# The mixer's indexer and recurrence, moved into the projections and the attention

## The reference, cut to what matters

```python
h = modulate(rmsnorm(x, mix_pre_g), m[3], m[4])
proj = h @ w_in
q, k, v, q_idx, k_idx, w_idx, x_lru, g_lru = split(proj)
# indexer: 8 heads of 64
score = einsum(relu(q_idx @ k_idx.T * 64 ** -0.5), w_idx * 8 ** -0.5)
score = where(admissible, score, -inf)        # causal by chunks of 64
top_idx = top_k(score, 64)                    # the keys each query may see
attn = softmax(q @ k.T / 8 + rel_bias, over the kept keys) @ v      # 8 heads of 64
# recurrence
xc = conv4(x_lru); r = sigmoid(xc @ w_a + b_a); i = sigmoid(xc @ w_i + b_i)
log_a = -8 * r * softplus(-lam); a = exp(log_a)
b = sqrt(-expm1(2 * log_a)) * i * xc
lru = scan(h = a * h + b) * gelu(g_lru)
merged = concat(rmsnorm(attn, attn_out_g), rmsnorm(lru, lru_out_g))
y = merged @ w_out
```

## Time and profile before

| what | us |
|---|---|
| median of 3 runs (3625.7 to 3627.49) | 3626.76 |
| the profiled execution's own time | 3632.07 |
| its span, first to last instruction | 3630.3 |
| projections' last product ends (start of span = 0) | 361.4 |
| attention's first product starts | 433.2 |
| output product starts | 482.5 |

### The profile page before, as it was taken

How to read it: one execution, slowest core, us unless ns; L and a number is a source line. 1 busy time by engine, 2 the same in 40 slices (tenths; PEclk the granted TensorE clock), 3 DMA queues, 4 the chain that set the end, 5 groups by cost and what they waited for, 6 DMA issues and landing times. The chain is left out here.

```text
span 3630.3 us, 55207 instructions
## 1 busy us (share of the span) xinstructions
PE 3347.6 (92%) x21195; PEld 3042.9 (84%) x21195; DVE 2466.5 (68%) x4014; ACT 1434.9 (40%) x1693; POOL 1078.2 (30%) x670
## 2 busy tenths in 40 slices
PE   6999479999798999989999999999988999999999
PEld 5989269957466899989999999997768999998887
DVE  5864737766575199998848998985663977106665
ACT  5433324312343333356633333323233457544443
POOL 0110000010000068766664334540000975660000
PEclk9999579989999999999999999998999999999999
DMA  7964026642002267789999999992103658867875
GB/s 297 337 244 180 0 93 223 241 151 103 24 1 90 73 210 265 255 271 364 362 328 402 378 378 410 409 356 82 58 24 140 213 189 254 266 224 283 304 281 210
DMA packets 305195, 814.35 MB, mean 224 GB/s; under 512 B 21760, under 2 KB 188928, under 8 KB 253696
## 3 DMA queue, kind: packets, MB, share of 16 engines
q1 hardware_dynamic: 241856, 583.07, 45.0%
q0 software_dynamic: 58752, 213.94, 15.8%
q10 hardware_dynamic: 4416, 15.05, 1.1%
HBM read 722.84 MB, written 89.13 MB: 224 GB/s over the span
## 5 line engine op out<-in xcount | busy, mean ns | idle before, releaser
L2521 POOL TENSOR_TENSOR arena_split<-ring,arena_split 128x1024 fp32r<-128x1024 f32 x256 | 643.5, 2525 | 1015.3 <-ACT arena_split L2475 1014.4
L2548 PE MATMUL ps<-xT_split,arena_split 128*128 128x384 f32 (+1 forms) x4096 | 916.6, 312 | 19.3 <-POOL arena_split L2521 11.4
L2548 PEld LDWEIGHTS ps<-xT_split,arena_split 128*128 128x128 f32 x4096 | 697.7, 191 | 20.3 <-issue 17.5
L2548 PE MATMUL ps<-hT_split,arena_split 128*128 128x384 f32 (+1 forms) x2048 | 635.1, 310 | 0.0
L2865 PE MATMUL ps<-arena_split 128*128 128x384 f32 x3072 | 535.7, 335 | 12.2 <-DVE arena_split L2817 12.1
L2865 PEld LDWEIGHTS ps<-arena_split 128*128 128x128 f32 x3072 | 534.2, 188 | 13.8 <-issue 12.0
L284 DVE TENSOR_TENSOR arena_split<-ring,arena_split 128x2048 fp32r<-128x2048 f32 x128 | 292.6, 2292 | 318.7 <-ACT arena_split L278 318.3
L2790 ACT ACTIVATE arena_split<-ring 128x2048 fp32r<-128x2048 f32 x128 | 245.5, 1918 | 477.1 <-PE ps L2865 282.7
L2548 PEld LDWEIGHTS ps<-hT_split,arena_split 128*128 128x128 f32 x2048 | 392.2, 191 | 0.0
L278 ACT ACTIVATE arena_split<-ring 128x2048 fp32r<-128x2048 f32 x128 | 244.0, 1912 | 351.0 <-PE ps L813 133.3
L2814 DVE TENSOR_TENSOR arena_split<-ring,arena_split 128x2048 fp32r<-128x2048 f32 x128 | 293.1, 2290 | 103.9 <-ACT arena_split L2790 103.7
(11 more groups left out here) (317 smaller groups left out, 5361.1 us busy)
## 6 DMA issues: line engine op xcount, KB each, us to landing
ring<-in_weights SPq DMA_DIRECT2D x396, 1024.0 KB, 5.3
arena<-in_side_weights POOLq DMA_DIRECT2D x152, 512.0 KB, 5.9
gates<-arena SPq DMA_DIRECT2D x48, 512.0 KB, 9.5
arena<-gates SPq DMA_DIRECT2D x32, 768.0 KB, 12.8
arena<-activations SPq DMA_DIRECT2D x64, 384.0 KB, 10.7
activations<-arena SPq DMA_DIRECT2D x128, 128.0 KB, 2.9
gates<-arena SPq DMA_DIRECT2D x16, 1024.0 KB, 6.9
arena<-gates SPq DMA_DIRECT2D x64, 256.0 KB, 5.0
```

The lines of the kernel that those rows point to most:

```text
L2521: pool.tensor_tensor(low, self.raw(f)[:, j, :], high.bitcast(F32), ALU.subtract)\
L2548: mm = pe.matmul(k.ps[:, j, 0:self.T], self.u[:, 2 * (f % 2) + j, a, t * P:(t + 1) * P], self.h[b][:, t, :], start=n == 0, stop=n == 3 * D ...
```

## The change

**The projections** take the chunks in the order 7, 8, 6, 4, 5, 9, 10, 0, 1, 2, 3: the recurrence's input, the indexer's keys, weights and queries, the gelu's input, and last q and k. SyncE loads them in that order, and the tiles of `proj` are renumbered. The loops over chunks are written out. On ScalarE `high(c + 2)` now stands ahead of the copy of chunk c. Behind chosen chunks each engine gets a slot of other work (c counts positions in the new order):

- TensorE: after c = 4 to 7 four indexer products each (after 4 also the small transposes), after c = 8 the eight gate products, into PSUM banks 4 to 7, which the projections do not use.
- ScalarE: the small exponential after c = 2, four relus each after 4 to 7, sigmoids after 8 and 9, the gelu after 10. It also copies v out, and then does tanh and exponential (`decays`).
- VectorE: half of the convolution behind `low(3)` and `low(4)`, softplus behind `low(5)`, four multiply-adds behind `low(6)` to `low(9)`, the rounds of largest values spread from `low(9)` on, and after `low(12)` the gates' scaling. Its last work in the stage is 3 rounds and the mask.

The relus have four buffers where they had two. The recurrence's tiles move to arena column 23040, the indexer's to 6656.

**The attention** takes the rest of the recurrence: VectorE does one piece at the end of steps 0, 1, 6, 7 to 10 (one scan of 256 columns each) and 11; ScalarE the square root after unit 6 and the squares after unit 14; TensorE the products with ones after the last unit. **TurnNormed** has the root, the reciprocal and the last four multiplications, and its end is signalled by VectorE after ScalarE's copies. The two stages Recurrence and Indexer are gone from the list.

```diff
 class Projections(Stage):
...
+    ORDER = (7, 8, 6, 4, 5, 9, 10, 0, 1, 2, 3)
...
+        for c in range(EARLY, self.CHUNKS):
             w.wait(pe, c)
-            pe.wait_ge(self.copied.sem, c + self.copied.at(-1))
+            pe.wait_ge(self.copied.sem, self.copied.at(c - 1))
...
+            if 4 <= c < 8:
+                pe.wait_ge(self.copied.sem, self.copied.at(c))
+                if c == 4:
+                    self.index.turn(pe)
+                self.index.products(pe, c - 4)
+            elif c == 8:
+                self.lru.gate_products(pe, self.index)
...
+        for c in range(self.CHUNKS):
+            w.wait_used(act, c)
+            w.high(act, c + 2, c + 2)
+            act.activation(self.proj[:, 2 * c:2 * c + 2, :].rearrange("p a t -> p (a t)"), k.ps[:, c % 2, :],
+                           ACT.Copy).then_inc(self.copied.sem, 1)
...
+        for c in range(EARLY, self.CHUNKS + 2):
+            w.low(dve, c, c)
+            if c in (3, 4):
+                dve.wait_ge(self.copied.sem, self.copied.at(c - 2))
+                lru.convolve(dve, c - 3)
+            elif c == 5:
+                lru.softplus(dve)
+            elif 6 <= c < 10:
+                index.add(dve, c - 6)
+                if c == 9:
+                    index.best_of(dve, 0, 0, 2)
+            elif c == 10:
+                index.best_of(dve, 0, 2, 6)
+            elif c == 11:
+                index.best_of(dve, 0, 6, 8)
+                index.best_of(dve, 1, 0, 2)
+            elif c == 12:
+                index.best_of(dve, 1, 2, 5)
+                lru.scale_gates(dve)
+        index.best_of(dve, 1, 5, 8)
+        index.mask(dve)
...
 class Recurrence:
...
+    def vector(self, dve, step):
+
+        t, chain = self.t, self.chain
+        if step == 0:
+            dve.wait_ge(self.acts.sem, self.acts.at(4))
+            chain(dve.tensor_tensor(t["sq"], t["a"], t["a"], ALU.mult))
+        elif step == 1:
+            dve.scalar_tensor_tensor(t["b"], t["sq"], 1.0, t["b"], ALU.add, ALU.mult).then_inc(self.steps.sem, 1)
+        elif step == 6:
+            dve.wait_ge(self.acts.sem, self.acts.at(5))
+            chain(dve.tensor_tensor(t["b"], t["b"], t["i"], ALU.mult))
...
+    def scalar(self, act, u):
+
+        t = self.t
+        if u == 6:
+            act.wait_ge(self.steps.sem, self.steps.at(3))
+            act.activation(t["b"], t["b"], ACT.Sqrt).then_inc(self.acts.sem, 1)
...
 class TurnNormed(Stage):
...
+        self.lru.out(dve)
+        self.finish(dve, (self.moved, 1))
```

More of the change, by code:

```diff
@@ L1001, in __init__, with begin @@
         self.sp = k.small[:, 16:64].rearrange("p (a b) -> p a b", b=4)
[L1003 to L1020, removed]
+    def begin(self, dve):
+        sp, lam = self.sp, self.k.col("lam")
+        chain = self.chain = Chain(dve, self.dve_chain)
         chain(dve.tensor_scalar(sp[:, 0, :], lam, -1.0, None, ALU.mult))
@@ L1036, in vector, with gate_products, sigmoids, gelu @@
         chain(dve.tensor_scalar(sp[:, 9, :], sp[:, 9, :], -8.0, None, ALU.mult))
+    def gate_products(self, pe, index):
+        k, t = self.k, self.t
+        pe.wait_ge(self.conv.sem, self.conv.at(1))
+        pe.wait_ge(k.late_load.sem, k.late_load.at(48))
+        pe.wait_ge(index.relus.sem, index.relus.at(16))
+        for g in range(2):
+            for c in range(4):
+                mm = pe.matmul(k.ps[:, 4 + 2 * g + c // 2, (c % 2) * SEQ:(c % 2 + 1) * SEQ], k.lru_w[:, g, c, :],
+                               t["xc"][:, c, :], start=True, stop=True)
+        mm.then_inc(self.gates.sem, 1)
+    def sigmoids(self, act, g):
+        k = self.k
+        if g == 0:
+            act.wait_ge(self.gates.sem, self.gates.at(1))
+        out, bias = self.t["ri"[g]], ("b_a", "b_i")[g]
+        for c in range(4):
+            last = act.activation(out[:, c, :], k.ps[:, 4 + 2 * g + c // 2, (c % 2) * SEQ:(c % 2 + 1) * SEQ], ACT.Sigmoid,
+                                  bias=k.col(bias, c, 1))
+        if g:
+            last.then_inc(self.acts.sem, 1)
+    def gelu(self, act):
+        act.activation(self.t["gelu"], self.gl, ACT.Gelu_apprx_tanh).then_inc(self.acts.sem, 1)
+    def scale_gates(self, dve):
+        t, sp = self.t, self.sp
         dve.wait_ge(self.acts.sem, self.acts.at(2))
@@ L1052, in vector @@
                 chain(ins)
[L1053 to L1059, removed]
@@ L1192, with __init__ @@
 class Attention(Stage):
-    def __init__(self, k, units, at, scale=None, turn=None, turned=None):
+    def __init__(self, k, units, at, scale=None, turn=None, turned=None, beside=None):
+        self.beside = beside
         self.k, self.s, self.units, self.scale, self.turn, self.buf = k, k.stage(), units, scale, turn, turned
@@ L1297, in tensor @@
                 value(step)
+        if self.beside:
+            self.beside.tensor(pe)
     def scalar(self, act):
@@ L3016, in program @@
         second_rest = turn(3, (2, 3, 4, 5), 7, layer=(1, 1))
+        lru = Recurrence(k)
         stages = [
@@ L3054, in _ @@
             def _(sp):
+                mixer = FIRST["w_in"]
                 def load(c, slot):
```

258 lines of the change are left out of this document (140 added, 118 removed).

## The result

The changed kernel takes 3572.84 us (median of 4 runs, 3569.48 to 3577.87) where the kernel before takes 3627.12 (4 runs): ratio 0.985 with a 95% interval of 0.983 to 0.986. Timed again in five rounds it took 3569.15, ratio 0.984 (0.982 to 0.985). Forecast were 3573.7 us, in a range of 3567.5 to 3582.5.

A forecast was written before the change was run, and what follows sets the result against it. TensorE sets the projections' pace, VectorE the serial recurrence and indexer. Attention starts 53.3 us earlier, the end loses 0.15: -53.1 takes the profiled 3632.07 to 3579.0, or 3573.7 after the 5.3 us median difference; range 3567.5 to 3582.5.

The forecast's parts named there:

- Index products: TensorE's 32 indexer passes, moved into the projections, add 7.2 us there, and the two small transposes 0.4.
- lower bound of 6.4: Least time for the index products in the projections: 32 passes at 0.20 us each, at 2.4 GHz.
- Gate products: TensorE's gate products, moved into the projections, take 3.4 us there, against 6.42 at the low clock; upper bound 6.4.
- Start: Chunk 2's first product comes at 296.4 instead of 296.90, gaining 0.5 us; the half clock up to 300 stays.
- Slots: Work behind each chunk fits the engines' free time, stalls zero; tightest `low(6)` and `low(12)`, about half a us to spare.
- the rival of the leaking slots: Projections: late `low` stalls TensorE 1 to 2 us, half clock adds 2.9; three slots cost 13, 3587; chance 0.1.
- Tail: VectorE's last run, from `low(11)` to the mask, takes 22.7 us; attention starts at 379.9 instead of 433.2, gaining 53.3.
- Attention: The recurrence's pieces beside the attention cost 0, bounds 0 and 12.1 us; it starts at 1.2 GHz as before.
- The rival's upper bound: Attention takes the pieces one behind the other: up to 8.5 + 3.6 = 12.1 us return, 3585.8; chance 0.08.
- End: After the attention, VectorE's last multiplications run beside transposes and ScalarE's moves; signalling through VectorE loses 0.15 us.
- The rival, given 0.2: Output product starts at full clock, raised by the products with ones: 2.5 us returns, 3571.2; chance 0.2.
- Sum: Whole program: -53.3 + 0.15 = -53.1 us, so the profiled 3632.07 us becomes 3579.0 and the median 3573.7.

The follow-up runs named there:

- The second profile of before: The kernel before, unchanged, once more under the profiler: 3620.86 us in its one run, 239.93 us from the early products' end to the feed-forward.

## Why the prediction was right

**What bounds.** TensorE's pace in the projections and VectorE's last run behind them, as forecast: with softplus doubled TensorE's wait passed on in full, and with the rounds placed earlier the attention came 6.4 us sooner.

**Index products.** Forecast 7.2 + 0.4 with the transposes, measured 1.47 + 3 x 1.25 = 5.2, 2.4 less. This is the term that was mis-sized, and it lies under the lower bound of 6.4. The bound took the time of a full-height pass for each; alternating heads lie on different halves of the partitions, and their passes overlap.

**Gate products.** Forecast 3.4, measured 3.44.

**Start.** Forecast 0.5 us earlier and the half clock kept as a cost; the gap was 1.54 us (c = 2 at 296.53) and the clock stayed at 1.00, which the profile of before had lost by chance. That is 1.5 us too little in the forecast against that profile, and none against an ordinary execution of before.

**Slots.** Forecast at no cost, and measured so. `low(6)` ended 2.3 us ahead of chunk 6's first product (317.72 + 2.29 against 322.29) and not half a us: I had counted VectorE's lateness, but not all of the time that the index products and transposes give. In the rival of the leaking slots, the price of a half clock was read wrong: chunk 2 ran at 0.50 for 3.1 us and lost 1.5, not 2.9. The real price of one late `low` is in the run with softplus twice, a stall of 2.85 and 1.6 of clock.

**Tail.** VectorE's last run was forecast at 22.7 us from `low(11)`; it took 22.2 (353.67 to 375.9). The terms named for it add up to 22.5.

**Attention.** Pieces at no cost: measured 0.14. The page on table loads of the Trainium skill (ScalarE: Activation LUTs, What ACT_TABLE_LOAD costs) would have added a drain of 1380 ns to each switch; the trace disagrees, with 1.31 us from the end of one function to the start of the next (389.80 to 391.11 and 392.17 to 393.48), of which the load is 1.28. The rival's upper bound was added too high: the pieces on VectorE are 4 x 1.22 + 2.44 = 7.3 us and not 8.5, so 10.9 in place of 12.1. What I missed is that the table which `decays` loads stays for the attention, 1.15 us.

**End.** Forecast 0.15 lost, measured 0.30 gained. The transposes at full clock gave 0.87, but the output product starts 2.23 us behind them where it started 1.66 behind them before: 0.57 lost. The forecast had VectorE's last multiplications run beside ScalarE's copies, and they end 0.5 us after them. Where the transposes were slow, with softplus twice, the copies ended last again and the signal cost 0.13, as forecast.

**The output product's clock.** The rival, given 0.2, came half true: the product began at 1.00 and fell to 0.50 after about 1.2 us. But 29.58 can't be called a gain of the change: with the products with ones it took 29.45 to 30.53 in seven profiles, without them 29.86 and 29.87, and in three profiles of the old order 29.53, 30.01 and 30.59.

**Sum.** Forecast 53.1. Against the first profile of before, the differences are 2.4 of index products, 0.4 of the tail, 1.5 of chunk 2's clock, 1.15 of the table, 0.45 at the end and 1.0 of the output product: 60.0, and the mixer measures 59.9. The second profile of before had kept chunk 2's clock, made the gate products in 1.0 less and the output product in 0.6 less: that takes 3.1 off, and 56.9 is what it measures. So the path and the overlaps were right, and the gain was put 3.8 us too low. That the time was forecast within 1 us of the first median is luck: 3626.76 less 56.9 would be 3569.9, near the second median, and the first lay 3.7 us above the second by the spread of stages that the change doesn't touch.

## What to carry to other kernels

When a serial stretch is moved beside a saturated engine, price three things apart: what the saturated engine gets, whether each slot fits the free time of the others, and the run of the last engine behind the final chunk. The last was the largest sum still to be had, and moving work from it to slots with measured idle brought the attention 6.4 us forward. When a stage between two others vanishes, look at the state that it left behind too, such as ScalarE's table.

## What the runs showed of the hardware that was not expected

- Float32 products of 64 rows that alternate between the halves of the partitions overlap on TensorE: eight passes of 256 columns in 1.07 us, against 1.93 when consecutive products use the same half, with a median of 376 ns for a pass in both.
- A gap of 2.03 to 2.04 us ahead of chunk 2 cost TensorE its full clock in one of three profiles of the old stages; gaps of 1.54 to 1.94 us kept it in nine of nine. Behind a stall of 2.85 us it was lost in the one profile with such a stall, and the half clock came only about 0.8 us after the products had resumed.
- The clock was kept at 1.00 from the products with ones over two gaps of 1.8 and 2.2 us with eight transposes between, and fell 1.2 us into the dense output product, in both profiles of the changed kernel. In four other kernels with the same code there the transposes ran at 1.00 and the output product began at 0.50; in a fifth both were at 0.50.
- The executions differ by up to 11 us in stages that are identical (3081.4 to 3092.8 us from the feed-forward's first product to the end). A difference of 3 us shown by a median of five runs is not safe here. A stretch whose clock doesn't change repeats far better: the attention took 40.25, 40.25, 40.25 and 40.23 us in four profiles, while the output product moved from 29.58 to 30.53.
